# Layer 0's gate and up products by Strassen's algorithm: seven products of a quarter each in place of eight, in fp32

## The reference

```
h = rms_norm(x, ffn_norm[l])
gate, up = jnp.split(h @ w_gate_up[l], 2, axis=-1)
x = x + ((jax.nn.silu(gate) * up) @ w_down[l]).astype(x.dtype)
```

## Time and profile before

| | |
|---|---|
| Median of 3 runs | 1885.32 us |
| The three runs | 1883.81, 1885.32, 1887.02 us |
| Span of the profiled execution | 1883.8 us |
| TensorE busy | 1836.7 us, 98% |
| TensorE weight loads busy | 924.5 us, 49% |
| VectorE busy | 667.3 us, 35% |
| ScalarE, GpSimd busy | 231.1 us, 208.4 us |
| Mean granted TensorE clock | 0.996 of full |
| DMA | 558.05 MB, mean 296 GB/s |

### The profile page before, as it was taken

The page is one execution under the profiler, slowest core; times in us unless marked ns, Lnnn a source line. Parts: engine busy times, 40 slices in busy tenths (PEclk is TensorE's granted clock), DMA queues, the critical chain, the costliest instruction groups (busy, mean ns, idle before and its releaser), DMA issues.

```text
span 1883.8 us, 22537 instructions
## 1 busy us (share of the span) xinstructions
PE 1836.7 (98%) x8210; PEld 924.5 (49%) x8211; DVE 667.3 (35%) x1416; ACT 231.1 (12%) x466; POOL 208.4 (11%) x399
## 2 busy tenths in 40 slices
PE   9999999999999999999999999999999999999997
PEld 4466777754667777675433333333333333333332
DVE  4553111135635774288431222122122122212222
ACT  1411000004211000123200101010010001000101
POOL 0200000002004867522000000000000000000000
PEclk9999999999999999999999999999999999999999
DMA  8143334242338784405699999999999699999995
GB/s 320 67 179 129 142 151 166 112 169 90 135 152 337 317 330 170 166 7 238 273 424 428 427 428 429 429 428 429 429 428 428 256 425 428 428 428 428 429 427 242
DMA packets 41177, 558.05 MB, mean 296 GB/s; under 512 B 4598, under 2 KB 5494, under 8 KB 6556
## 3 DMA queue, kind: packets, MB, share of 16 engines
q1 hardware_dynamic: 40396, 556.06, 71.5%
q10 hardware_dynamic: 720, 1.18, 0.2%
HBM read 556.16 MB, written 1.06 MB: 296 GB/s over the span
## 4 chain that ended last, share of the span: by engine, by line
PE 68%; DMA 22%; DVE 7%; ACT 1%; issue 1%; DVEq 0%; SPq 0%; ACTq 0%; POOLq 0%
DMA mega<-in_exp_w 17%; PE PS L1823 16%; PE PS L2135 12%; PE PS L1842 8%; PE PS L2175 7%; PE PS L1547 7%; DMA tenth<-in_exp_w 5%; PE PS L1724 3%; PE PS L2121 2%; PE PS L2019 1%; PE PS L1865 1%; PE PS L1859 1%; PE PS L2128 1%; PE PS L1518 1%; DVE tmp L1434 1%
## 5 line engine op out<-in xcount | busy, mean ns | idle before, releaser
L2135 PE MATMUL PS<-mega,tb 128*64 128x512 f32 x1728 | 378.2, 593 | 8.1 <-POOLq L2299 7.5
L1823 PE MATMUL PS<-hT,mega 128*128 128x256 f32 x1376 | 300.6, 379 | 0.0
L1823 PEld LDWEIGHTS PS<-hT,mega 128*128 128x128 f32 x1376 | 261.1, 190 | 43.0 <-issue 8.6
L2135 PEld LDWEIGHTS PS<-mega,tb 128*64 128x64 f32 x1728 | 123.5, 137 | 257.3 <-issue 239.1
L1434 DVE TENSOR_SCALAR tmp<-PS 128x512 f32<-128x512 f32 x34 | 23.5, 692 | 547.6 <-PE PS L2135 547.6
L2175 PE MATMUL PS<-mega,tb 128*64 128x512 f32 x896 | 198.4, 595 | 0.0
L1547 PE MATMUL PS<-mega,hT 128*128 128x512 f32 (+2 forms) x416 | 171.1, 551 | 0.0
L1842 PE MATMUL PS<-mega,late 128*128 128x512 f32 x352 | 154.7, 593 | 0.0
L2175 PEld LDWEIGHTS PS<-mega,tb 128*64 128x64 f32 x896 | 61.9, 137 | 133.1 <-issue 130.6
L1137 DVE TENSOR_TENSOR late<-PS,late 128x512 f32<-128x512 f32 x22 | 15.2, 691 | 269.9 <-PE PS L1823 269.9
L1842 PEld LDWEIGHTS PS<-mega,late 128*128 128x128 f32 x352 | 66.6, 190 | 76.3 <-issue 75.6
(11 more groups left out here) (464 smaller groups left out, 1706.3 us busy)
## 6 DMA issues: line engine op xcount, KB each, us to landing
mega<-in_exp_w SPq DMA_DIRECT2D x154, 2048.0 KB, 25.9
mega<-in_w_gate_up SPq DMA_DIRECT2D x22, 2048.0 KB, 8.0
tenth<-in_exp_w SPq DMA_DIRECT2D x19, 2048.0 KB, 29.1
late<-in_exp_w SPq DMA_DIRECT2D x19, 2048.0 KB, 27.6
mega<-in_ada_w SPq DMA_DIRECT2D x12, 2048.0 KB, 9.0
mega<-in_w_down SPq DMA_DIRECT2D x10, 2048.0 KB, 7.3
mega<-in_w_in_part SPq DMA_DIRECT2D x9, 2048.0 KB, 10.7
mega<-in_w_out SPq DMA_DIRECT2D x6, 2048.0 KB, 8.2
```

The source lines that it names most:

```text
L1823: ins = pe.matmul(PS[:, 4 + 2 * (i % 2) + part, 256 * f:256 * f + 256], wt[:, k, 256 * part + 128 * f:256 * part + 128 * f + 128], hT[:, k ...
L2135: ins = pe.matmul(PS[64 * h:64 * h + 64, b, :], xg[:, o:o + 64], slot_of(r, s)[:, w:w + 512], start=False, stop=k == KC - 1, skip_group_ch ...
```

## The change

In layer 0, blocks 1 to 10 (`FAST_LAYERS = 1`), gate and up are computed together as one product of 2 x 2 quarters: the tokens' side `hs` (first scaled by `rows_R`) is cut into token tiles and halves of the inner dimension (`a11` to `a22`), the weight block into halves of the inner dimension and gate/up (`b11` to `b22`). Seven products of quarters, each 8 matmuls of 128x128 by 128 columns, replace the eight quarter products that lay in 32 matmuls of 256 columns. VectorE forms four sums of weights for each block (128x1024 each, one in place), and once for the layer `hs` and four sums of tokens. ScalarE copies three of the products out of PSUM (`e1`, `e6`, `e5`) before the next product is accumulated into the same bank; VectorE adds those copies to what stands in PSUM. Banks 4, 5 and 6 serve every block, where before two pairs took turns. Block 0 stays as it was, except that gate and up report separately and up lands in bank 7. In layer 1 only the values of semaphores change; several semaphores elsewhere are merged into others to make room.

```diff
+FAST_LAYERS = 1
+FIRST, SIXTH, FIFTH, SEVENTH, THIRD, SECOND, FOURTH = range(1, 8)
...
+        hs = mega[:, 4096 * RING:4096 * RING + TT * D].rearrange("p (k t) -> p k t", k=KC)
+        tok = [[hs[:, 4 * kh:4 * kh + 4, P * t:P * t + P] for kh in range(2)] for t in range(TT)]
```

ScalarE, blocks 1 to 10 of layer 0:

```diff
+                        for j, (product, bank, copy) in enumerate(((FIRST, 4, e1), (SIXTH, 6, e6), (FIFTH, 5, e5))):
+                            act.wait_ge(g.p_p, 7 * n + product)
+                            if j == 0 and n >= 1:
+                                act.wait_ge(g.e_x, n)
+                            link.to(nc.scalar.activation(copy, PS[:, bank, 0:256], ACT.Copy), g.e_e, 3 * n + j + 1)
+                        act.wait_ge(g.p_p, 7 * n + SECOND)
+                        act.wait_ge(g.s_actv, l * FF_BLOCKS + i)
+                        link.to(nc.scalar.activation(th_T[:, 0:256], PS[:, 4, 0:256], ACT.Tanh, scale=0.5), g.s_th, l * (2 * FF_BLOCKS - 1) + 2 * i)
+                        act.wait_ge(g.s_gr, l * FF_BLOCKS + i + 1)
+                        act.sem_inc(freed[PLACE[("gu", i), l][0]], 1)
+                        link.to(nc.scalar.activation(th_T[:, 256:512], gate_1, ACT.Tanh, scale=0.5), g.s_th, l * (2 * FF_BLOCKS - 1) + 2 * i + 1)
```

VectorE; `weight_sums` is called for block 1 between the token sums of block 0, and for each later block at the end of the block before it:

```diff
+                def weight_sums(i, which):
...
+                    if 1 in which:
+                        slot, use = PLACE[("gu", i), l]
+                        v.wait_ge(landed[slot], 16 * use + 16)
+                        link.to(v.tensor_tensor(wsum1, b12, b11, ALU.subtract), g.t_w, n + 1)
+                        link.to(v.tensor_tensor(wsum2, b22, wsum1, ALU.subtract), g.t_w, n + 2)
+                    if 3 in which:
+                        link.to(v.tensor_tensor(b12, b22, b12, ALU.subtract), g.t_w, n + 3)
+                        link.to(v.tensor_tensor(wsum4, b21, wsum2, ALU.subtract), g.t_w, n + 4)
+                def fast_block(i):
...
+                    v.wait_ge(g.e_e, 3 * n + 2)
+                    link(v.tensor_tensor(p16, e1, e6, ALU.add))
+                    v.wait_ge(g.p_p, 7 * n + SEVENTH)
+                    link.to(v.tensor_tensor(p167, PS[:, 6, 0:256], e1, ALU.add), g.s_v, n + 1)
+                    v.wait_ge(g.e_e, 3 * n + 3)
+                    link(v.tensor_tensor(us1, p167, e5, ALU.add))
+                    v.wait_ge(g.p_p, 7 * n + THIRD)
+                    link(v.tensor_tensor(us0, PS[:, 5, 0:256], p16, ALU.add))
...
+                    link.to(v.tensor_tensor(gate_1, PS[:, 6, 0:256], e1, ALU.add), g.s_gr, l * FF_BLOCKS + i + 1)
...
+                    if i + 1 < FF_BLOCKS:
+                        weight_sums(i + 1, (1, 3))
```

TensorE:

```diff
+                def fast_block(i):
...
+                    def product(left, right, bank, first):
+                        for f in range(2):
+                            for k in range(4):
+                                ins = pe.matmul(PS[:, bank, P * f:P * f + P], right[:, k, P * f:P * f + P], left[:, k, :],
+                                                start=first and f + k == 0, stop=not first and k == 3, skip_group_check=True)
+                        ins.then_inc(g.p_p, 1)
...
+                    product(a11, b11, 4, True)
...
+                    product(tsum2, wsum2, 6, True)
...
+                    product(tsum1, wsum1, 5, True)
...
+                    pe.wait_ge(g.e_e, 3 * n + 2)
+                    product(tsum3, b12, 6, False)
...
+                    pe.wait_ge(g.e_e, 3 * n + 3)
+                    product(tsum4, b22, 5, False)
+                    product(a12, b21, 4, False)
+                    pe.wait_ge(g.t_w, 4 * n + 4)
+                    pe.wait_ge(g.s_v, n + 1)
+                    product(a22, wsum4, 6, False)
```

More of the change, by code:

```diff
@@ L569, in _ @@
                 act.wait_ge(g.s_rb, l + 1)
-                link.to(nc.scalar.activation(rows_R, PS[:, 7, 0:256], ACT.Copy), g.s_re, l + 1)
+                link.to(nc.scalar.activation(rows_R, PS[:, 5 if l < FAST_LAYERS else 7, 0:256], ACT.Copy), g.s_re, l + 1)
                 for i in range(FF_BLOCKS):
+                    if l < FAST_LAYERS and i >= 1:
+                        n = l * (FF_BLOCKS - 1) + i - 1
+                        for j, (product, bank, copy) in enumerate(((FIRST, 4, e1), (SIXTH, 6, e6), (FIFTH, 5, e5))):
[9 more added lines that the diff above has]
+                        link.to(nc.scalar.activation(th_T[:, 256:512], gate_1, ACT.Tanh, scale=0.5), g.s_th, l * (2 * FF_BLOCKS - 1) + 2 * i + 1)
+                        if i % 2 == 0:
+                            act.wait_ge(g.s_dn, l * FF_BLOCKS + i)
+                            act.sem_inc(freed[PLACE[("dn", (i - 1) // 2), l][0]], 1)
+                        continue
                     act.wait_ge(g.s_gr, l * FF_BLOCKS + i + 1)
@@ L574, in _ @@
                         act.wait_ge(g.s_actv, l * FF_BLOCKS + i)
[L575 removed]
+                    link.to(nc.scalar.activation(th_T, gs_T[i % 2], ACT.Tanh, scale=0.5), g.s_th, l * (2 * FF_BLOCKS - 1) + i + 1)
                     if i % 2 == 0 and i >= 2:
@@ L1132, in _ @@
                 for i in range(FF_BLOCKS):
                     n = l * FF_BLOCKS + i
-                    v.wait_ge(g.s_gu, n + 1)
+                    if l < FAST_LAYERS and i >= 1:
+                        fast_block(i)
+                        continue
+                    v.wait_ge(g.s_gu, blocks_before(l) + i + 1)
+                    if l < FAST_LAYERS:
+                        gp, upp = (PS[:, 4 + 3 * j, :].rearrange("p (f t) -> p f t", f=2) for j in range(2))
+                        link.to(v.tensor_tensor(gs_T[0].rearrange("p (f t) -> p f t", f=2), gp, rows, ALU.mult), g.s_gr, n + 1)
+                        m = 5 * l
+                        link.to(v.tensor_tensor(hs, hT[:, :, :], rows_R.unsqueeze(1).broadcast_to([P, KC, T]), ALU.mult), g.h_s, m + 1)
+                        link.to(v.tensor_tensor(tsum1, tok[1][0], tok[1][1], ALU.add), g.h_s, m + 2)
+                        link.to(v.tensor_tensor(tsum2, tsum1, tok[0][0], ALU.subtract), g.h_s, m + 3)
+                        weight_sums(1, (1,))
+                        link.to(v.tensor_tensor(tsum3, tok[0][0], tok[1][0], ALU.subtract), g.h_s, m + 4)
+                        link.to(v.tensor_tensor(tsum4, tok[0][1], tsum2, ALU.subtract), g.h_s, m + 5)
+                        weight_sums(1, (3,))
+                        v.wait_ge(g.s_gv, l + 1)
+                        v.sem_inc(freed[PLACE[("gu", i), l][0]], 1)
+                        link.to(v.tensor_tensor(us_T.rearrange("p (f t) -> p f t", f=2), upp, rows, ALU.mult), g.s_pf, blocks_before(l) + 1)
+                        v.wait_ge(g.s_th, l * (2 * FF_BLOCKS - 1) + 1)
+                        link(v.scalar_tensor_tensor(gs_T[0], th_T, 1.0, gs_T[0], ALU.add, ALU.mult))
+                        link.to(v.scalar_tensor_tensor(act_T[0], gs_T[0], 0.5, us_T, ALU.mult, ALU.mult), g.s_actv, n + 1)
+                        continue
@@ L1812, in _ @@
                         for part in range(2):
+                            bank = 4 + 3 * part if fast else 4 + 2 * (i % 2) + part
                             for f in range(2):
@@ L1822, in _ @@
                                 for k in range(KC):
-                                    ins = pe.matmul(PS[:, 4 + 2 * (i % 2) + part, 256 * f:256 * f + 256], wt[:, k, 256 * part + 128 * f:256 * part + 128 * f + 128],
+                                    ins = pe.matmul(PS[:, bank, 256 * f:256 * f + 256], wt[:, k, 256 * part + 128 * f:256 * part + 128 * f + 128],
                                                     hT[:, k, :], start=k == 0, stop=k == KC - 1)
+                            if fast and part == 0:
+                                ins.then_inc(g.s_gu, 1)
                             if i == 0 and part == 0:
@@ L1841, in _ @@
                                     ft = 2 * c + f
-                                    ins = pe.matmul(PS[:, 2 * t + nh, :], act_T[c % 2][:, 256 * f + 128 * t:256 * f + 128 * t + 128],
+                                    o = 256 * t + 128 * f if fast and c >= 1 else 256 * f + 128 * t
+                                    ins = pe.matmul(PS[:, 2 * t + nh, :], act_T[c % 2][:, o:o + 128],
                                                     wd[:, ft % 4, 512 * nh:512 * nh + 512], start=ft == 0, stop=ft == FF_TILES - 1)
```

94 lines of the change are left out of this document (67 added, 27 removed).

## The result

The changed kernel takes 1871.65 us (median of 4 runs, 1870.68 to 1872.31), the kernel before, in the same comparison, 1885.22 us (4 runs, 1883.81 to 1887.02): a ratio of 0.9928, with a 95% interval of 0.9914 to 0.9942. Forecast were 1872.3 us, in a range of 1868.5 to 1878.7. In a second comparison of the same two kernels the medians are 1872.81 (5 runs) and 1885.70 us (15 runs), again 0.9928 (0.9915 to 0.9942). The gain of the medians is 13.6 us in the one and 12.9 us in the other; 13.0 was forecast.

A forecast was written before the change was run, and what follows sets the result against it. TensorE alone bounds the changed stage, 20.68 us a block. Saving 1.30 us in each of blocks 1 to 10 takes 13.0 from 1883.8, giving 1870.8; the median's 1.5 above makes 1872.3 us, range 1868.5 to 1878.7.

The forecast's parts named there:

- The price of the passes: Layer 0, blocks 1 to 10: 112 passes at 0.1117 us replace 64 at 0.2158, gaining 1.30 us a block, 13.0 in all.
- E: Rival: TensorE's granted clock falls in the ten changed blocks, which would lose 130 us: 2002 us, chance 0.02.
- The margins: Fast blocks: copies and sums are ready before the products needing them, with margins of 1.0 to 3.7 us.
- Block 0: Layer 0's first block, preparing the token side: sums ready near 184.0, sixth product reached at 185.0, margin 1.0 us.
- VectorE's busy time: Layer 0: rises by about 60 us, ten blocks at 5.3 and some 10 in the first block.
- The gain reaches the end: Experts' weight stream moves with the work ahead of it, so the 13.0 us carry through to the end.
- B: Rival: two of seven product starts in each block wait, 0.23 us each, losing 4.6 us: 1877 us, chance 0.06.
- C: Rival: seven flagged product starts a block cost more than the eighth saved: 1895 us; chance 0.03 slower, 0.02 within 0.2%.
- D: Rival: the gain stays hidden behind a DMA transfer, leaving 1885 us, chance 0.03.

The follow-up runs named there:

- The eight narrow products: Kernel before, with gate and up matmuls of layer 0's blocks 1 to 10 cut into 128-column halves, no Strassen: 1889.88 us, ratio 1.0021.
- the late copy: Changed kernel with four idle ScalarE operations ahead of the copy of the sixth product: 1880.36 us, 0.9974 of before.

## Why the prediction was right

**The price of the passes** was right: 0.1117 us a pass forecast and measured, 12.51 us a block, 1.30 us gained in each of ten blocks. The eight narrow products show that it is the price of the shape and comes with no Strassen. The reason given for it, that the weight load sets the pace, no experiment varied; it rests on rows of the profile before. With 128 weight columns the passes start 0.112 us apart at 128 moving columns and no closer at 64. With 64 weight columns and 30 moving ones, the chain of waits has 64 passes in 3.85 us, 0.060 us each:

```profile
99.01 3.85 PE PS L1627 x64
```

So the spacing follows the weight columns and not the moving ones in these three shapes; at 256 moving columns, with 0.2158 us a pass, it no longer does. The milestones of the two chains show the 13 us arriving. The residual addition behind the stage starts at 396.93 us before and at 383.57 now, 13.4 earlier, of which 0.3 were already there ahead of the stage. The second run of 16 passes in layer 1's block 0 starts at 556.65 in the earlier trace rows, and now, in the chain of waits:

```profile
542.98 2.02 PE PS L1951 x16
```

That is 13.7 us earlier. By the estimate that the prediction made from the section "Back-to-back issue gap" of the Trainium skill's page "TensorE: Matmul & The Clock Gate" a pass would have cost 0.133 us; the stage, with its 0.1117 over 1120 passes, disagrees. The section "Why this matters for your kernels" of the Trainium skill's same page lets thin matmuls make the clock oscillate, unless the loop takes all slices of the inner dimension before it waits for the next transfer. This kernel's loops do that, one wait for a whole weight block, and the granted clock was 1.00 from 168 to 384 us. The trace agrees with the rule, and the prediction's "by that rule E would happen" left its condition out.

**The margins** were right to 0.2 us in the fast blocks. With T = 202.08: the sixth was to be copied out at T+4.2 (it was T+4.21), the fifth at T+6.1 (T+6.0), the sum over the seventh at T+7.9 (T+7.83); the activation was to be ready at T+14.9 (216.98, T+14.90), the second weight sum 3.7 us ahead of its product (3.7). "Without it (down products moved away) the sixth product would wait about 3.2 us" was not tried by itself, but delays of 2.5, 5.0 and 6.2 us gave waits of none, 1.29 and 2.56 us.

**Block 0** was the one place that I mis-sized, and its forecast was met in part by luck. Timelines of VectorE and GpSimd there:

```profile
176.66 1.28 POOL L2345 TENSOR_TENSOR par<-par,K 128x512 f32<-128x512 f32 x1 [94.42 <-DMA par<-in_layer_params]
177.19 2.90 DVE L1213 TENSOR_TENSOR mega<-hT,late 128x2048 f32<-128x2048 f32 x1
180.12 0.69 DVE L1214 TENSOR_TENSOR tenth<-mega 128x512 f32<-128x512 f32 x1
...
182.83 1.23 DVE L1174 TENSOR_TENSOR tenth<-mega,tenth 128x1024 f32<-128x1024 f32 x1
```

And in the second profile of the changed kernel:

```profile
177.70 2.29 DVE L1213 TENSOR_TENSOR mega<-hT,late 128x2048 f32<-128x2048 f32 x1
177.88 3.24 POOL L2345 TENSOR_TENSOR par<-par,K 128x512 f32<-128x512 f32 x1 [95.12 <-DMA par<-in_layer_params]
180.03 1.64 DVE L1214 TENSOR_TENSOR tenth<-mega 128x512 f32<-128x512 f32 x1
```

The scaling of hT, estimated at 2.44 us from the 1024-element row, took 2.90 in the first profile and 2.29 in the second. What differs is one operation of GpSimd, which takes 1.27 us in the profile before, where VectorE does nothing beside it. Where it starts ahead of the scaling, it keeps its 1.28 us and the scaling is 0.6 us longer. Where it starts behind the scaling's start, the scaling takes 2.29, GpSimd's operation 3.24 and the token sum behind the scaling 1.64 in place of 0.69 us, 0.95 longer. So it is in all eight traces of the changed kernel and its variants: two of the first kind, six of the second. The two engines hold each other up here; that is read from these timelines, no run moved the operation.

In the first profile the second weight sum was ready at 184.06, as forecast (184.0), since a chain of sums that began 0.3 us earlier than I had it made up for part of the scaling. ScalarE's copy at its head ended at 176.38, 0.28 us earlier than in the earlier trace rows. TensorE too reached the sixth product earlier, at 184.49 rather than 185.0: the whole stage begins 0.3 us earlier in this execution, and a chain's row begins some 0.16 us behind the first pass's start. The margin is 0.4 us, not 1.0. In the second profile the sum is ready at 184.91, where its product was due at 185.00 and started at 185.06: no margin is left, and the block takes 12.64 us. With the sums of the later blocks delayed by two and by four operations, where this block's own sums are untouched, it takes 12.63 and 12.65, and there too the product starts 0.15 us behind the sum's end. "Margin 1.0 us, and a miss costs its size once" was right only in that the loss comes once and is small, 0.13 us.

**VectorE's busy time** rose by 65.4 us, not 60: a fast block runs seven operations of 256 columns, of which I had counted six, so it adds 2.97 + 0.69 + 4.9 - 2.76 = 5.8 us and ten add 58; the scaling and four token sums of block 0 add 2.90 + 2.76 = 5.7. That makes 63.7; the last 1.7 us I have not traced. The error has no effect on the path.

**The gain reaches the end**, as forecast: the experts' chain keeps its 29.3 us a load, and the first load of 29.30 us in it stands 15.3 us earlier (1172.11 against 1187.36 in the earlier trace rows):

```profile
1172.11 29.30 DMA mega<-in_exp_w
```

That is 2 us more than the change gave, as is the profiled span, 1868.6 against 1883.8. I do not count these 2 us as the change's. They go with short stretches at a granted clock of 0.50 behind 780 us, which fall differently from one execution to the next: 3.4 us long, at 796, 891.6 and 935.9 us in the profile before, only at 911.5 in this one, and at 783.5 and 913.2 in the second profile of the changed kernel (all three profiles also end at 0.50, from 1877.7, 1859.9 and 1861.5 us). Up to 779 us, where there are none, the shift between the two profiles is 13.4 to 13.7 us; it is 15.6 us at 879, 16.1 at 928 and 15.2 at the end. In the second profile, with two such stretches, the shift against the profile before is 13.1 us at 779 and 14.6 at the same load. The medians, 13.6 and 12.9 us apart, are the better measure.

**The rivals.** B (starts that have to be served, 0.23 us each) did not occur, but for the one start of 0.13 us in block 1; its price was measured by the late copy as 0.20 us. C, the other side, had the right kind of reason and the wrong place: a product start costs nothing while its flag is up, and with all seven served late at 0.20 us a block would have lost 1.4 us against a gain of 1.30, that is no change. The other side that the runs did find is another one: VectorE's sums late by 5 us give the gain back, and 1.2 us more make it 1.3% slower than before, since the clock then falls. I had the cover (the down products, 6.87 us) but not the clock's part in the price of losing it. D and E did not occur, and no wait of VectorE for a weight load stands in the stage's list of waits.

## What to carry to other kernels

Price a replaced matmul by the start-to-start spacing of back-to-back passes of exactly its shape, weight load included; if the kernel has such a run of passes anywhere, its chain gives the total to a per cent. A one-level Strassen then gains an eighth of the narrow cost and pays first for the narrowing: here 1.78 less 0.48 us a block. Place each product whose result is copied back as an operand so that one whole product runs in between, put the sums under work that does not need them, and read the margin of each; a margin lost costs more than its length.

## What the runs showed of the hardware that I had not expected

- The clock's answer to a gap. Behind nine gaps of 1.29 us it stayed at 1.00; behind gaps of 2.56 us it fell to 0.50 for 3.4 us in eight of nine, and the passes' spacing went from 0.112 to 0.213 us, starting a microsecond after TensorE had resumed. Between these it is not settled: in the profile before it fell behind 2.35 us without a pass; behind the same wait, in the changed kernel's first profile, it didn't, and in its second it did (the first's timeline, then window with the columns of the earlier trace rows):

```profile
782.41 1.09 PE L1988 MATMUL PS<-K,mega 128*128 128x128 f32 x8 [2.35 <-ACT mega L631]
```

```profile
782.40:785.80 3.40, 2.92 (x13) 1.62 (x14) 1.74 (x11) 3.11 (x7) 0.00 (x0) 1.00 0.00 0
```

- The idle time that the groups show understates a wait: 0.63 us shown was 0.87 us on the path, and 1.29 shown was 1.52, for the reasons given with the late copy.
- One operation of GpSimd and one of VectorE that overlap in time lengthen each other: 128x512 on GpSimd took 1.27 us by itself and 3.24 behind VectorE's scaling, and VectorE lost 0.6 or 0.95 us, by which of them had started first. In block 0 that decided whether the sixth product found its sum ready.
